# Two units' products with the rounded activations in front of both units' products with the rests, at the head of the split expert units

## The reference, cut to what matters

```
q = (xc @ w_q).reshape(-1, PEER_HEADS, 2, half)
s = jnp.einsum('thpd,pkd->thpk', q, sub_keys)
sv, si = lax.top_k(s, PEER_TOPK)          # then 16 of the 16x16 sums, their ids and a softmax g
...
a = jax.nn.gelu(jnp.einsum('td,thkd->thk', xc, ue))
return jnp.einsum('thk,thkd->td', (g * a).astype(ve.dtype), ve)
```

## Time and profile before

| | |
|---|---|
| median of 3 runs | 3236.11 us (3229.24, 3236.11, 3247.51) |
| profiled execution, its own time | 3233.33 us |
| its span, first to last instruction | 3231.5 us |
| mean granted TensorE clock | 0.988 |
| PE busy | 3133.4 us (97% of the span) |
| DVE busy | 2305.6 us (71%) |
| ACT busy | 1625.5 us (50%) |
| POOL busy | 684.1 us (21%) |

### The profile page before, as it was taken

One profiled execution on the slowest core, in us unless ns is written; L12 is line 12 of the kernel. 1 busy time (PEld: TensorE's weight loads), 2 busy tenths in 40 slices (PEclk: granted clock), 3 DMA queues, 4 the chain that ended last, 5 costly groups with the idle time before them and its releaser, 6 DMA issues.

```text
span 3231.5 us, 61306 instructions
## 1 busy us (share of the span) xinstructions
PE 3133.4 (97%) x21286; PEld 2840.7 (88%) x21286; DVE 2305.6 (71%) x4210; ACT 1625.5 (50%) x3026; POOL 684.1 (21%) x678
## 2 busy tenths in 40 slices
PE   6999999999999999999999999999999999999998
PEld 5779999988887866899999888889988999998998
DVE  6549988877777345898887777777667767766754
ACT  1224578854444254456886444454454445445443
POOL 0107745520000000484553000000010010000000
PEclk9999999999999989999999999999999999999999
DMA  7635555468886322455435788878643886854353
GB/s 284 241 129 171 187 165 167 162 223 266 263 262 222 122 92 69 147 185 167 136 136 188 244 262 262 266 245 275 212 158 130 277 279 207 271 188 134 128 185 118
DMA packets 176627, 632.22 MB, mean 196 GB/s; under 512 B 23624, under 2 KB 23632, under 8 KB 175728
## 3 DMA queue, kind: packets, MB, share of 16 engines
q1 hardware_dynamic: 134416, 491.48, 45.3%
q0 software_dynamic: 42064, 139.07, 13.1%
q10 hardware_dynamic: 16, 0.01, 0.0%
HBM read 627.21 MB, written 9.50 MB: 197 GB/s over the span
## 4 chain that ended last, share of the span: by engine, by line
PE 89%; DVE 5%; ACT 2%; DMA 1%; DVEq 1%; issue 1%; ACTq 0%; SPq 0%; POOL 0%
PE ps L687 21%; PE ps L528 13%; PE ps L529 12%; PE ps L530 12%; PE ps L516 6%; PE ps L668 3%; PE ps L666 3%; PE ps L667 3%; PE ps L563 2%; PE ps L1080 2%; PE ps L1079 2%; PE ps L882 1%; PE ps L578 1%; PE ps L787 1%; DMA ring<-stream 1%
## 5 line engine op out<-in xcount | busy, mean ns | idle before, releaser
L1615 DVE TENSOR_TENSOR unit_low<-ring,unit_high 128x1024 fp32r<-128x1024 f32 x484 | 643.7, 1330 | 164.5 <-ACT unit_high L1167 156.3
L1167 ACT CAST unit_high<-ring 128x1024 fp32r<-128x1024 f32 x528 | 552.1, 1046 | 223.7 <-PE ps L530 165.8
L530 PE MATMUL ps<-expert_x_high,unit_low 128*128 128x256 f32 x1968 | 549.7, 279 | 0.0
L528 PE MATMUL ps<-expert_x_high,unit_high 128*128 128x256 f32 x1552 | 446.3, 288 | 1.6 <-DVE unit_low L1615 1.4
L529 PE MATMUL ps<-expert_x_low,unit_high 128*128 128x256 f32 x1552 | 434.1, 280 | 0.0
L530 PEld LDWEIGHTS ps<-expert_x_high,unit_low 128*128 128x128 f32 x1968 | 369.2, 188 | 0.0
L687 PE MATMUL ps<-unit_low,expert_high 128*128 128x512 f32 x1024 | 323.5, 397 | 2.2 <-DVE unit_low L1615 2.2
L687 PE MATMUL ps<-unit_high,expert_low 128*128 128x512 f32 x1024 | 320.8, 394 | 0.1
L687 PE MATMUL ps<-unit_high,expert_high 128*128 128x512 f32 x1024 | 319.1, 393 | 1.2 <-ACT unit_high L1167 1.2
L528 PEld LDWEIGHTS ps<-expert_x_high,unit_high 128*128 128x128 f32 x1552 | 293.3, 189 | 6.9 <-issue 2.2
L529 PEld LDWEIGHTS ps<-expert_x_low,unit_high 128*128 128x128 f32 x1552 | 291.5, 188 | 0.0
(11 more groups left out here) (348 smaller groups left out, 7682.6 us busy)
## 6 DMA issues: line engine op xcount, KB each, us to landing
ring<-stream SPq DMA_DIRECT2D x754, 512.0 KB, 3.9
arena<-stream SPq DMA_DIRECT2D x160, 512.0 KB, 4.3
score<-ada POOLq DMA_DIRECT2D x128, 512.0 KB, 5.1
arena<-ada POOLq DMA_DIRECT2D x96, 512.0 KB, 5.1
arena<-bias_tiles POOLq DMA_DIRECT2D x48, 192.0 KB, 2.7
arena<-ada SPq DMA_DIRECT2D x8, 1024.0 KB, 17.4
bias_tiles<-bias_rows POOLq DMA_DIRECT2D x8, 768.0 KB, 14.9
x_home<-x POOLq DMA_DIRECT2D x2, 1024.0 KB, 6.5
```

What stands on the lines that cost most here:

```text
L528: pe.matmul(out, hi[:, kt, :], xh[:, kt, :], start=(kt == 0), stop=False)
L530: mm = pe.matmul(out, lo[:, kt, :], xh[:, kt, :], start=False, stop=(kt == KD - 1))
L1167: nc.scalar.copy(hi, raw_of(unit)).then_inc(whi_ready, 1)
L1615: V.tensor_tensor(out=lo, in0=raw_of(unit), in1=hi, op=ALU.subtract).then_inc(wlo_ready, 1)
```

## The change

`expert_first` takes units 4 and 5 together. PE multiplies unit 4 by `xhi` (16 matmuls, bank `ps[0]`), then unit 5 by `xhi` (16 matmuls, bank `ps[1]`), then unit 4 by `xlo` (8, with the waits for `xlo_ready`), then unit 5 by `xlo` (8). The waits for the gelu that empties the bank and for the low part of unit 5 stand now in front of its first 16 matmuls. `unit_done` is still signalled once for each unit, behind its last product with `xlo`. Unit 5 no longer goes through `expert`. No instruction is added or left out; both expert layers are changed alike.

```
-                    out = ps[k % 2][:, 0:S]
-                    hi, lo = (w.rearrange("p (k n) -> p k n", k=KD) for w in parts_of(u + k, n + k))
-                    pe.wait_ge(gelu_ready, NE * l + k + 1)
+                    parts = [[w.rearrange("p (k n) -> p k n", k=KD) for w in parts_of(u + k + e, n + k + e)] for e in range(2)]
                     pe.wait_ge(xhi_ready, xhi0[ph] + 4)
-                    pe.wait_ge(wlo_ready, n + k + 1)
-                    for kt in range(KD):
-                        pe.matmul(out, hi[:, kt, :], xhi[:, kt, :], start=(kt == 0), stop=False)
-                        pe.matmul(out, lo[:, kt, :], xhi[:, kt, :], start=False, stop=False)
-                    for kt in range(KD):
-                        if kt % 2 == 0:
-                            pe.wait_ge(xlo_ready, xlo0[ph] + kt // 2 + 1)
-                        mm = pe.matmul(out, hi[:, kt, :], xlo[:, kt, :], start=False, stop=(kt == KD - 1))
-                    mm.then_inc(unit_done, 1)
+                    for e, (hi, lo) in enumerate(parts):
+                        out = ps[(k + e) % 2][:, 0:S]
+                        pe.wait_ge(gelu_ready, NE * l + k + e + 1)
+                        pe.wait_ge(wlo_ready, n + k + e + 1)
+                        for kt in range(KD):
+                            pe.matmul(out, hi[:, kt, :], xhi[:, kt, :], start=(kt == 0), stop=False)
+                            pe.matmul(out, lo[:, kt, :], xhi[:, kt, :], start=False, stop=False)
+                    for e, (hi, lo) in enumerate(parts):
+                        out = ps[(k + e) % 2][:, 0:S]
+                        for kt in range(KD):
+                            if e == 0 and kt % 2 == 0:
+                                pe.wait_ge(xlo_ready, xlo0[ph] + kt // 2 + 1)
+                            mm = pe.matmul(out, hi[:, kt, :], xlo[:, kt, :], start=False, stop=(kt == KD - 1))
+                        mm.then_inc(unit_done, 1)
...
-                for k in range(NPLAIN + 1, NPLAIN + 4):
+                for k in range(NPLAIN + 2, NPLAIN + 4):
                     expert(k)
```

## The result

The reordered kernel takes 3251.56 us, median of 9 runs (3244.68 to 3269.15), against 3233.07 us for the kernel before in 9 runs (3223.14 to 3247.51): a ratio of 1.0063, 95% interval 1.0040 to 1.0087. That is 18.5 us slower, outside the predicted 3226 to 3246 us and over the 0.5% that was given 0.04. The nine runs fall into two groups, five from 3244.7 to 3251.6 us and four from 3260.5 to 3269.2 us. The profiled execution is one of the upper group: 3261.68 us, 28.4 us over the 3233.33 us of the profiled execution before.

A forecast was written before the change was run, and what follows sets the result against it. PE, busy for 97% of the span, was taken to bound the kernel; gains of 0.97 and 1.27 us in the two layers, 2.24 us together, gave 3233.9 us for the median, taken as 3234 us, range 3226 to 3246 us.

The forecast's parts named there:

- the 0.5% that was given 0.04: Whole kernel: chance 0.04 of being slower by over 0.5%, about 16 us; within 0.5% was given 0.93.
- no new wait arises at unit 5: Unit 5's 16 moved matmuls find the gelu of unit 3 (254.04) and their low part (253.95) ready.
- unit 4's end: Unit 4 ends when it did, within 0.1 us; 0.7 of PE's 2.26 us stall remain before its last two matmuls.
- the 1.89 us at unit 6: 16 matmuls moved into the stall let unit 6 start at 259.82 and not at 261.71.
- the ring keeps a part: Unit 8's load waits for unit 4's end, so 0.9 us and 0.6 us of the two layers' gains are lost.
- unit 8's gain in the first layer: PE gets unit 8 at 266.39 where it was at 267.36: 0.97 us won.
- the wait at the end of the routing: In front of unit 58, PE's wait stays at some 1.2 to 1.5 us and the gain passes.
- The stretch from unit 4 to unit 58: From unit 4's start to unit 58's start, each layer is to be 0.9 to 1.3 us shorter.
- DVE comes along: At the second exponential, DVE goes at POOL's pace and comes earlier with PE, so all the layer's gain remains.
- rival 3: DVE misses a turn before the second exponential, its L2160 ending one unit later; costs 2.9 us, 3239.0 us; chance 0.22.
- rows 8: Eight additions before the second exponential, one per POOL instruction, bring DVE and POOL back into step some 17 us before.
- rival 4: PE's clock falls to 1.2 GHz after its changed pauses, a 2.83 us unit taking up to twice that; 0.03 with anything else.

The follow-up runs named there:

- e1: The reordered kernel with POOL's long memset of the arena made to wait until ACT has taken the second exponential; 3230.8 us, ratio to the kernel before 0.9993.
- e2: The kernel before, in its old order, with POOL's long memset made to wait for the second exponential; 3232.64 us, ratio 1.0001.
- e5: The reordered kernel with the long memset cut in two, the second half waiting until behind the second exponential; 3244.99 us, ratio to the kernel before 1.0024.
- e6: The reordered kernel with the long memset issued as eight back-to-back pieces of 8 units each, no added wait; 3241.63 us, ratio to the kernel before 1.0046.
- e7: The reordered kernel with four dummy matmuls behind the reorder, giving back 0.8 us of its 1.9 us gain; 3250.26 us, ratio to the kernel before 1.005.
- e3: The reorder in the first expert layer alone, the second layer as in the kernel before; 3244.11 us, ratio to the kernel before 1.0021.
- e9: The kernel before, unchanged, run for one more profile; 3251.31 us.

## Why the prediction was wrong

**Right:** that no new wait arises at unit 5; unit 4's end (PE's wait fell to 0.5 us a layer, 0.7 worked out); the 1.89 us at unit 6 (1.83 measured); that the ring keeps a part, and unit 8's gain in the first layer (1.10 us, 0.97 worked out; in the second 0.80 us, 1.27 worked out); the wait at the end of the routing, which shifts with PE and stayed at 1.3 us. With the memset out of the way the reorder's median lies 1.8 us lower (e1 against e2), within the scatter of both. The profiles don't bear out a gain either. The stretch from unit 4 to unit 58, which was to be 0.9 to 1.3 us shorter, takes 160.08 and 159.51 us in e1's two layers against 158.61 and 159.00 us in the profile before. Of the reordered layers in which PE doesn't wait for the gelu only the second ones of e5 and e6 are shorter, 158.53 and 158.00 us.

**Wrong, first step: "DVE comes along".** The step was that DVE's small instructions go at POOL's pace, so that an advance of PE is handed on to it. At the head the opposite happened. In the kernel before, one of the instructions from L2155 to L2160 is blocked by a low part in the first half of the routing, and it ends at 271.98:

```profile
269.49 2.49 DVE L2160 TENSOR_TENSOR pick<-pick,small 128x128 f32<-128x128 f32 x1
```

In the reordered kernel POOL makes the low parts of the units 8 to 11 without a gap, and two are blocked:

```profile
264.00 4.76 POOL L2332 TENSOR_TENSOR unit_low<-ring,unit_high 128x1024 fp32r<-128x1024 f32 x2 [0.91 <-ACT unit_high L1170]
268.70 4.79 POOL L2332 TENSOR_TENSOR unit_low<-ring,unit_high_early 128x1024 fp32r<-128x1024 f32 x2
268.77 2.45 DVE L2158 TENSOR_SCALAR r_ab<-r_ci 128x128 uint32<-128x128 uint32 x1
271.13 2.38 DVE L2160 COPY small<-pick 128x8 f32<-128x8 f32 x1
273.80 0.28 DVE L2163 TENSOR_TENSOR pick<-pick,small 128x128 f32<-128x128 f32 x1
```

L2163 ends at 274.08, 2.1 us later. The gap is missing because unit 8's load hangs on unit 4's end, which didn't move, while the loads of the units 9 to 11 came earlier: counted from unit 4's start, ACT's high parts of the units 8 to 11 begin 0.03, 0.58, 0.97 and 1.37 us earlier than before, those of 8, 9 and 10 released by the transfer. It is the same ring that kept a part of the gain. In this layer DVE doesn't regain the turn. The eight additions end at 356.50 where they ended at 354.38, and the cast at the second exponential begins 2.4 us later than its like before (373.62 against 371.18), while POOL's last low part begins 0.6 us earlier (373.55 against 374.12):

```profile
371.18 0.30 DVE L2159 CAST pick<-r_ab 128x256 f32<-128x256 uint32 x1
...
374.12 2.81 POOL L2329 TENSOR_TENSOR unit_low<-ring,unit_high_early 128x1024 fp32r<-128x1024 f32 x1 [0.39 <-ACT unit_high_early L1167]
376.87 13.81 POOL L2404 MEMSET arena<- 128x16384 f32 x1
```

The case was rival 3, which named this mechanism and the point from which it decides, L2160 ending later than 374.1 us; it had 0.22. Against it I held that rows 8 bring the two back into step, and here they don't bring back a whole turn. The reading of these rows was off as well: four of the eight additions take 2.6 us and four 0.4 us, so DVE makes two for each POOL instruction and not one.

The turn lost at the head makes DVE late more often, but it doesn't settle it. In all eleven profiled layers with the reorder and a full or half advance (those of the reordered kernel, e1, e5, e6 and e7 and the first of e3; line numbers as in the reordered kernel) the first half's L2163 ends 20.1 to 21.3 us behind unit 4's start, where L2160 ended at about 18.7 us in the three profiles of the kernel before that show no long wait. In eight of the eleven DVE then begins the second half's L2157 at 118.7 us or later, where L2154 began at 116.6 to 116.9 us before; seven of these were caught, and the eighth is e1's, whose memset waits. In the other three, the second layers of e1, e5 and e6, it begins at 110.3 to 117.0 us, and PE doesn't wait for the gelu. The caught layer of e9 goes the other way: its head is on time (18.74 us), and DVE loses its turn at a pair of additions of L2173, which begins at 281.44 and takes 5.03 us where its like before took 2.83 us. The 100 us between the head and the exponential have a part in it that no run isolates.

**Wrong, second step: the price of a missed turn.** Rival 3 put it at one unit of 2.83 us, 2.9 us for both layers. Its sum stopped at the low part that DVE waits for and left out what POOL has queued behind the last one: the memset, 13.75 us, issued without a wait as soon as the low part of unit 47 is made. Measured, a missed turn there costs 14.9 to 15.4 us of waiting and 2.5 us (first layer) or 1.6 us (second) of clock, and e5 shows the price to be the memset's length. That term, sized 1.6 and 1.3 us where the two layers lose 16.8 and 16.5 us, is why even the range missed. The clock's part, the 0.50 behind the pause, was rival 4's mechanism, but it came as a consequence of the long pause and not of the changed short ones.

**What could have been read.** The memset stands in the page's source order behind the last low part, and in the timeline of the kernel before it starts at 376.87, 3.0 us behind L2160's end. And the three runs of the kernel before, 18 us apart, were taken for scatter: in e9 an execution at 3251 us is one with a caught cast. A spread that nothing in the profile explains is itself a row to be read.

The Trainium skill ("SBUF — State Buffer", section "Who interferes with whom") states both halves of what is seen here: a copy, cast or tensor_scalar in a two-port mode and a GpSimd instruction exclude each other for the whole instruction, while a DVE instruction with two inputs in SBUF is held up by a GpSimd instruction that reads SBUF, not by one that only writes. The traces agree: cast and tensor_scalar stand through the memset (16.16, 14.65 us), and in the kernel before the low part that DVE makes at 378.54, with two inputs, takes its 1.23 us beside it. In which mode an instruction ran no row shows.

**What stays open:** why the turn is lost in some executions of the kernel before, in which the order of work is the same, and made good in some layers of the reordered one (no run here isolates what differs); and the two longest runs of e6.

## What to carry to other kernels

Where instructions of two engines shut each other out, as DVE's cast and POOL's memset do here, look at the longest instruction that either has queued behind the point where they meet, and not only at the one that is running: that was the price of a cast that began 0.07 us behind a low part. Let a long fill of the one wait for the small critical instruction of the other; here one wait (e1, e2) takes away the long executions of both kernels and costs nothing that can be measured. A small gain at the head of a pipeline with a ring can move the first units less than the later ones, as here, and so close the gaps through which another engine works: follow that engine to its next deadline before counting the gain.

## What the runs showed of the hardware that was not expected

A blocked DVE cast did not get its turn between POOL's low part and the memset right behind it: it stood through both, 16.16 us. So did the tensor_scalar L2157 in the second layer, which began while the low part was running (14.65 us). In the first layer of e6 the same instruction, begun beside the last low part in the same way, did get through between it and the first piece of the memset (1.15 us), and DVE got through again behind the first and the second piece, of about 1.8 us each. What decides between the two no run shows. A copy of 128x8 elements, 0.16 us when free, is blocked for 2.38 us like a large one.
